# Routing products of a PEER layer: four fp32 matmuls per group of four tokens become twelve bf16 matmuls

## The reference, cut to what matters

```python
experts = i1 * PEER_NKEYS + i2
g = jax.nn.softmax(top_s.astype(jnp.float32), axis=-1)
u = expert_u[ec]
act = jax.nn.gelu(jnp.einsum('cd,ced->ce', xc, u).astype(jnp.float32))
return jnp.einsum('ce,ced->cd', gc * act, expert_v[ec])
```

## Time and profile before

| | |
|---|---|
| median of 3 runs | 1339.16 us |
| the profiled execution | 1341.18 us |
| its span, first to last instruction | 1339.4 us |
| PE busy | 1248.0 us, 93% |
| DVE, ACT, POOL busy | 836.9, 713.1, 564.2 us |
| granted TensorE clock, mean | 0.969 of full speed |
| HBM read and written | 235.36 and 13.11 MB |

### The profile page before, as it was taken

How to read it: one execution, slowest core, us unless ns; L and a number is a source line. 1 busy time by engine, 2 the same in 40 slices (tenths; PEclk the granted TensorE clock), 3 DMA queues, 4 the chain that set the end, 5 groups by cost and what they waited for, 6 DMA issues and landing times.

```text
span 1339.4 us, 26686 instructions
## 1 busy us (share of the span) xinstructions
PE 1248.0 (93%) x8546; PEld 1143.3 (85%) x8546; DVE 836.9 (62%) x1812; ACT 713.1 (53%) x1473; POOL 564.2 (42%) x500
## 2 busy tenths in 40 slices
PE   7979989978898888999999999999999999999996
PEld 6968878976786688999999999999988888888885
DVE  4595766977535544799445555553076767676765
ACT  5435667433545544555664444545555655555554
POOL 2653453532325723788886666667900000000000
PEclk8999999988898988999999999999999999999998
DMA  6575655564453423455555556565757565757552
GB/s 215 168 234 165 221 178 189 191 241 149 167 195 111 142 98 123 156 178 185 172 173 178 186 174 189 179 190 180 259 190 251 203 243 196 252 190 257 195 190 92
DMA packets 85471, 249.35 MB, mean 186 GB/s; under 512 B 7931, under 2 KB 29563, under 8 KB 84508
## 3 DMA queue, kind: packets, MB, share of 16 engines
q1 hardware_dynamic: 77212, 209.69, 47.0%
q0 software_dynamic: 8192, 38.80, 8.3%
HBM read 235.36 MB, written 13.11 MB: 186 GB/s over the span
## 4 chain that ended last, share of the span: by engine, by line
PE 80%; DVE 9%; ACT 4%; issue 3%; POOL 2%; DMA 2%; DVEq 0%; ACTq 0%; SPq 0%
PE psum L626 79%; DVE s_sb L1519 2%; POOL arena L1449 2%; DMA arena<-mods 1%; ACT w_hi L1049 1%; DVE w_lo L1510 1%; ACT arena L1186 1%; PE psum L789 1%; DVE arena L1739 1%; DVE rstd L1504 1%; DVE arena L1625 1%; DMA par<-params 0%; DVE h_lo L1632 0%; DVE h_lo L1546 0%; ACT arena L1032 0%
## 5 line engine op out<-in xcount | busy, mean ns | idle before, releaser
L1049 ACT ACTIVATE w_hi<-ring 128x512 fp32r<-128x512 f32 x734 | 453.6, 631 | 400.9 <-PE psum L626 394.7
L1383 POOL TENSOR_TENSOR w_lo<-ring,w_hi 128x512 fp32r<-128x512 f32 x367 | 483.7, 1321 | 306.5 <-ACT w_hi L1049 294.1
L626 PE MATMUL psum<-h_hi,w_hi 128*128 128x256 f32 x1832 | 540.2, 295 | 44.1 <-DVE w_lo L1510 18.5
L626 PE MATMUL psum<-h_lo,w_hi 128*128 128x256 f32 x1832 | 523.9, 286 | 0.0
L626 PE MATMUL psum<-h_hi,w_lo 128*128 128x256 f32 x1832 | 523.6, 286 | 0.0
L626 PEld LDWEIGHTS psum<-h_hi,w_hi 128*128 128x128 f32 x1832 | 356.8, 195 | 63.9 <-issue 37.3
L626 PEld LDWEIGHTS psum<-h_lo,w_hi 128*128 128x128 f32 x1832 | 357.8, 195 | 0.3
L626 PEld LDWEIGHTS psum<-h_hi,w_lo 128*128 128x128 f32 x1832 | 356.8, 195 | 0.0
L1510 DVE TENSOR_TENSOR w_lo<-ring,w_hi 128x512 fp32r<-128x512 f32 x239 | 182.1, 762 | 138.6 <-ACT w_hi L1049 138.4
L626 PE MATMUL psum<-w_hi,h_hi 128*128 128x512 f32 (+1 forms) x592 | 224.2, 379 | 6.2 <-DVE arena L1527 5.4
L626 PE MATMUL psum<-w_hi,h_lo 128*128 128x512 f32 (+1 forms) x592 | 222.9, 377 | 0.0
(11 more groups left out here) (183 smaller groups left out, 1016.9 us busy)
## 6 DMA issues: line engine op xcount, KB each, us to landing
ring<-u_t SPq DMA_DIRECT2D x128, 512.0 KB, 3.5
ring<-v_rows SPq DMA_DIRECT2D x128, 512.0 KB, 3.5
ring<-weights SPq DMA_DIRECT2D x115, 512.0 KB, 4.0
arena<-mods POOLq DMA_DIRECT2D x48, 512.0 KB, 4.6
routing_weights<-s_sb SPq DMA_DIRECT2D x32, 320.0 KB, 4.2
s_sb<-routing_weights POOLq DMA_DIRECT2D x5, 2048.0 KB, 9.2
bias_rows<-arena POOLq DMA_DIRECT2D x1, 1536.0 KB, 5.9
xres<-x_t SPq DMA_DIRECT2D x1, 1024.0 KB, 4.8
```

What stands on the lines that cost most here:

```text
L626: return nc.tensor.matmul(out, lhs, rhs, start=start, stop=stop, **kw)
L1049: nc.scalar.activation(w_hi[:, half, :], src, ACT.Copy).then_inc(hi_done, 1)
L1383: nc.gpsimd.tensor_tensor(w_lo[:, half, :], src, w_hi[:, half, :].bitcast(F32), ALU.subtract)\
```

## The change: what it does

The routing products are done in bf16. A one-hot row is exact in bf16. The weight is cut into three bf16 pieces that add up to it, so that G = hot1^T x wgt0 + hot1^T x wgt1 + hot1^T x wgt2, accumulated in PSUM: twelve bf16 matmuls a quad, each with 128 columns of weights and 128 moving columns. Once, after the indices are turned, DVE makes the three pieces of all weights in seven instructions; two of them stay in PSUM bank 5, the third goes to SBUF. For each quad DVE makes hot2 (a new table with a one at `i2`) and hot1, and multiplies hot2 by the first and the second piece: four instructions on four tokens each, of which all read an operand in PSUM. ACT multiplies hot2 by the third piece, one instruction a token (`third_weights`), between the gelu and the copy of its step. PE waits for one semaphore more before a quad, and ACT waits for hot2.

```diff
-        hot1 = flat(112, 4).rearrange("p (b t k) -> p b t k", b=2, t=4)
-        wgt = flat(116, 4).rearrange("p (b t k) -> p b t k", b=2, t=4)
-        sel_2, sel_w = s_sb[:, 0:T], s_sb[:, T:2 * T]
+        def quad_pair(region):
+            return region.bitcast(BF16).rearrange("p (b t k) -> p b t k", b=2, t=4)
+
+        hot1, hot2 = quad_pair(flat(112, 2)), quad_pair(flat(114, 2))
+        wgt = [quad_pair(r) for r in (flat(116, 2), flat(118, 2), s_sb[:, 2304:2816])]
+        sel_1, sel_2 = psum[:, 4, 0:T], psum[:, 4, T:2 * T]
+        sel_w = [psum[:, 5, T * x:T * x + T] for x in range(2)]
+        sel_w2, high_part, rest = (s_sb[:, T * x:T * x + T] for x in (0, 2, 3))
+        piece = s_sb[:, T:T + T // 2].bitcast(BF16)
@@ PE
             def quad(s, q, first):
                 pe_.wait_ge(hot1_ready, q + 1)
                 pe_.wait_ge(wgt_ready, q + 1)
+                pe_.wait_ge(wgt2_ready, q + 1)
                 if not first:
                     pe_.wait_ge(g_read, q - 3)
                 for j in range(4):
-                    last = mm(psum[:, GBANKS[s], j * P:j * P + P], hot1[:, s % 2, j, :], wgt[:, s % 2, j, :], True, True)
+                    for x in range(3):
+                        last = mm(psum[:, GBANKS[s], j * P:j * P + P], hot1[:, s % 2, j, :], wgt[x][:, s % 2, j, :], x == 0, x == 2)
                 last.then_inc(route_done, 1)
@@ ACT
+            act.wait_ge(sel_read, 6)
+
+            def third_weights(s, q):
+                act.wait_ge(hot2_ready, q + 1)
+                for t in range(4):
+                    col = sel_w2[:, 4 * q + t:4 * q + t + 1] if isinstance(q, int) else sel_w2[:, bass.ds(q * 4 + t, 1)]
+                    last = nc.scalar.activation(wgt[2][:, s % 2, t, :], hot2[:, s % 2, t, :], ACT.Copy, scale=col)
+                last.then_inc(wgt2_ready, 1)
...
                 for s in range(4):
                     high_u(s, it * 4 + s, False)
                     gelu(s + 2, it * 4 + s - 2)
+                    third_weights(s, it * 4 + s - POOL_TILES)
                     copy_quad(s, it * 4 + s - first, it - first // 4)
@@ DVE
-            v.tensor_copy(sel_2, psum[:, 4, T:2 * T]).then_inc(sel_read, 1)
-            v.tensor_copy(sel_w, psum[:, 5, 0:T]).then_inc(sel_read, 1)
+            v.tensor_copy(piece, sel_w[0]).then_inc(sel_read, 1)
+            dve.wait_ge(sel_read, 1)
+            v.tensor_copy(high_part, piece).then_inc(sel_read, 1)
             dve.wait_ge(sel_read, 2)
+            v.tensor_tensor(rest, sel_w[0], high_part, ALU.subtract).then_inc(sel_read, 1)
+            dve.wait_ge(sel_read, 3)
+            v.tensor_copy(sel_w[0], high_part)
+            v.tensor_copy(piece, rest).then_inc(sel_read, 1)
+            dve.wait_ge(sel_read, 4)
+            v.tensor_copy(sel_w[1], piece).then_inc(sel_read, 1)
+            dve.wait_ge(sel_read, 5)
+            v.tensor_tensor(sel_w2, rest, sel_w[1], ALU.subtract).then_inc(sel_read, 1)
+            dve.wait_ge(sel_read, 6)
...
             def one_hots(q):
                 if q >= 2:
                     dve.wait_ge(route_done, q - 1)
-                rows = iota[:, :].unsqueeze(1).to_broadcast([P, 4, P])
-                v.tensor_tensor(hot1[:, q % 2, :, :], rows, bc(psum[:, 4, 4 * q:4 * q + 4].unsqueeze(2), [P, 4, P]), ALU.is_equal)\
-                    .then_inc(hot1_ready, 1)
-                for t in range(4):
-                    at = 4 * q + t
-                    last = v.tensor_scalar(wgt[:, q % 2, t, :], iota[:, :], sel_2[:, at:at + 1], sel_w[:, at:at + 1],
-                                           ALU.is_equal, ALU.mult)
+                v.tensor_tensor(hot2[:, q % 2, :, :], rows, spread(sel_2, q), ALU.is_equal).then_inc(hot2_ready, 1)
+                v.tensor_tensor(hot1[:, q % 2, :, :], rows, spread(sel_1, q), ALU.is_equal).then_inc(hot1_ready, 1)
+                dve.wait_ge(hot2_ready, q + 1)
+                for x in range(2):
+                    last = v.tensor_tensor(wgt[x][:, q % 2, :, :], hot2[:, q % 2, :, :], spread(sel_w[x], q), ALU.mult)
                 last.then_inc(wgt_ready, 1)
```

More of the change, by code:

```diff
@@ L377, in block_program @@
         wgt_ready = sem("wgt_ready")
+        hot2_ready = sem("hot2_ready")
+        wgt2_ready = sem("wgt2_ready")
         early_weighted = sem("early_weighted")
@@ L1292, in _ @@
             nc.scalar.activation(blk(106), blk(106), ACT.Exp).then_inc(soft_exp, 1)
-            u_loop(SOFT_TILE, POOL_TILES + COPY_LAG)
-            act.wait_ge(sel_done, 1)
+            u_loop(SOFT_TILE, POOL_TILES)
+            act.wait_ge(sel_read, 6)
[5 more added lines that the diff above has]
+                last.then_inc(wgt2_ready, 1)
+            for s in range(COPY_LAG):
+                high_u(s, POOL_TILES + s, False)
+                gelu(s + 2, POOL_TILES + s - 2)
+                third_weights(s, s)
             def copy_quad(s, q, more):
@@ L1307, in _ @@
                 gelu(s + 2, first + s - 2)
+                third_weights(s, COPY_LAG + s)
                 copy_quad(s, s, None)
-            with act.Fori(first // 4 + 1, (first + QUADS) // 4) as it:
+            with act.Fori(first // 4 + 1, (POOL_TILES + QUADS) // 4) as it:
                 for s in range(4):
@@ L1312, in _ @@
                     gelu(s + 2, it * 4 + s - 2)
+                    third_weights(s, it * 4 + s - POOL_TILES)
                     copy_quad(s, it * 4 + s - first, it - first // 4)
+            for s in range(COPY_LAG):
+                n = POOL_TILES + QUADS + s
+                high_u(s, n, False)
+                gelu(s + 2, n - 2)
+                copy_quad(s, n - first, (n - first) // 4)
             u_loop(first + QUADS, P)
@@ L1889, in _, with spread @@
             dve.wait_ge(sel_done, 1)
-            v.tensor_copy(sel_2, psum[:, 4, T:2 * T]).then_inc(sel_read, 1)
-            v.tensor_copy(sel_w, psum[:, 5, 0:T]).then_inc(sel_read, 1)
+            v.tensor_copy(piece, sel_w[0]).then_inc(sel_read, 1)
+            dve.wait_ge(sel_read, 1)
+            v.tensor_copy(high_part, piece).then_inc(sel_read, 1)
             dve.wait_ge(sel_read, 2)
+            v.tensor_tensor(rest, sel_w[0], high_part, ALU.subtract).then_inc(sel_read, 1)
[7 more added lines that the diff above has]
+            dve.wait_ge(sel_read, 6)
+            def spread(row, q):
+                return bc(row[:, 4 * q:4 * q + 4].unsqueeze(2), [P, 4, P])
+            rows = iota[:, :].unsqueeze(1).to_broadcast([P, 4, P])
             def one_hots(q):
```

## The result

The changed kernel takes 1327.63 us (median of 4 runs, 1326.21 to 1329.58) against 1339.68 of before, 12.05 us less; the ratio of the runs is 0.9915 with a 95% interval of 0.9901 to 0.9929. Forecast were 1328.2 us and 11.0 us less, within 1322 to 1345. In a second comparison it took 1328.42 (6 runs) against 1339.05 (19 runs): 0.9922, 0.9906 to 0.9938. All ratios are of undisturbed executions; two of the kernel before, of 2436 and 3942 us, stay out of them.

The account below looks back on a forecast made before the run. PE was taken to bound the kernel: 64 quads at 0.72 instead of 0.89 us save 11.0, the helpers cost nothing. 1341.18 profiled becomes 1330.2, and with the median 2.0 lower, 1328.2 us; range 1322 to 1345.

Parts of the forecast that it names:

- PE sets the pace, and the saving of a quad comes out whole: In the stage from 676.09 us, PE time saved is saved at the end: quad 0.89 to 0.72, 11.0 us in all.
- The price of a pair, 0.060: On PE, one bf16 matmul costs 0.0533 for its columns plus 0.0068; 12 make a quad of 0.72 us.
- fp32r's fixed part: On PE, 0.0135 us of each fp32r matmul beyond its columns; half, 0.0068, was taken for bf16.
- The bounds, columns alone and all of the fixed part: PE's quad at 0.64 us, saving 16.2, with none of the fixed part; at 0.80, saving 5.8, with all.
- VectorE is covered, by 0.75 a step: DVE needs 2.85 us a quad against PE's step of 3.60, so its added work costs nothing.
- the 0.2 for waits: Allowance in DVE's sum per quad, about 0.2 us for the two waits it can meet.
- rival 3: DVE products at 1.05 need 3.76 a step, or ACT above 3.7; time stays 1339; 12% together with a pair near 0.074.
- ScalarE's wait and its lag: ACT idles 1 us for hot2, third pieces add 1.2, high parts start late, POOL ends about 1 us later; cost nothing.
- Once per kernel: DVE prepares the pieces in seven instructions, 2.9 instead of 0.8 us, hidden by five tiles before quad 0.
- Rivals 1 and 2: PE's bf16 weight loads cost 0.112 each, as fp32 (1368 us, 15%), or go by bytes, 0.079 (1342.7 us, 9%).
- What was to show it: Timeline signs: quad near 0.72, step near 3.60, DVE idle about 0.8, ACT waiting about 1 us, chain one piece of PE.

Follow-up runs that it names:

- the half-column kernel: The changed kernel with the second and third piece multiplied for only 64 of 128 moving columns; 1316.84 us against 1338.04 of the kernel before, 0.9831.
- the kernel without this lag: The changed kernel with the third weighted piece made by VectorE instead of ScalarE; 1327.44 us against 1339.05 of the kernel before, 0.993.

## Why the prediction was right

*PE sets the pace, and the saving of a quad comes out whole.* Right: a quad holds PE 0.159 less and the step is 0.153 shorter, 9.8 us in the stage, and the kernel with the new tables but fp32 matmuls gains nothing. The median fell by 12.05 where 11.0 were forecast, and by 10.6 in the second comparison; how near 1328.2 the first came is in part the spread of executions.

*The price of a pair, 0.060.* The sum was right, the working only in part, and that it came out is luck. The pair costs 0.056: the 0.0533 of the columns and hardly anything more. I had added half of fp32r's fixed part, 0.0068, with the reason that bf16 weights have half the bytes; what is there is 0.003, and the half-column kernel shows that the load of bf16 weights, at most 0.028, is not what bounds the pair. Against that, I had nothing for the crossing between fp32r and bf16, which is 0.06 a quad: 0.054 at its end, where the last matmul holds PE for 0.110 instead of 0.056, and 0.01 at its start. Rows 5 had the figure that fits the end, 0.112 for a load that nothing hides, but I looked for it only in the quad's own loads. 12 x 0.004 too much and 0.062 too little nearly cancel: 0.72 forecast, 0.734 measured, 11.0 us forecast and 9.8 in the stage. The bounds, columns alone and all of the fixed part, held.

One reading in it is less certain than it was put: that the fp32 quad was bound by its loads and not by its columns. The kernel before also has fp32 matmuls with 256 moving columns on 128 weight columns:

```profile
219.71 4.55 PE L626 MATMUL psum<-arena,ring 128*128 128x256 f32 x20 [0.18 <-ACT arena L1032]
...
219.71 4.99 PE L626 MATMUL psum<-arena,ring 128*128 128x256 f32 x22 [0.18 <-ACT arena L1032]
```

These are two views of one stretch, and two records more are 0.44: about 0.22 a record (0.216 by the records). If such a record goes by its columns, 128 of them take half of it, 0.108, nearly the 0.112 of the load, so the rows leave open which of the two bound the quad. The forecast does not use it, as a bf16 pair escapes both.

The Trainium skill's page "TensorE: Matmul & The Clock Gate", section "Back-to-back issue gap", has 56 ns for the matmul alone and 81 ns for the pair of load and matmul; this trace agrees with the first (0.056) and not with the second, although every one of these matmuls has its own load of weights. The other rule weighed, the fast load for weights that are not fp32 (section "Weight-path perf modes"), fits the 0.028 measured with 64 moving columns, where fp32 records with 128 weight columns and only 8 moving ones take 0.112.

*VectorE is covered, by 0.75 a step.* Right: 0.87 left, and the four table instructions run at 0.68 like hot1. Of the 0.2 for waits half was needed: 3.61 - 0.87 is 2.74, beside the 2.64 of the instructions. With two products more DVE's own step is 3.85 and the gain is gone, so rival 3 was a real one, two instructions away. Its price, 1.05 for a product with two SBUF operands, came from a misread row; where such a product did run beside POOL, it took 1.04, of which about 0.36 is time that it waited and could spare, so the step held. How much more than this DVE could carry was not tried.

*ScalarE's wait and its lag.* Right in kind and size: 0.70 of waiting where I had 1.0, third pieces of 1.28 where I had 1.2, the high parts late by about a microsecond and POOL with them, and nothing of it reaches PE, whose step is the same in the kernel without this lag.

*Once per kernel.* In the timeline of DVE the seven instructions take 3.1 us and are hidden: from the first matmul that turns the indices to the first quad are 15.04 us in the traces before and after.

*Rivals 1 and 2*, a load bound at 0.112 or 0.079 a pair, are refuted by the pairs of 0.056 and 0.028.

*What was to show it* came as said in the quads, the step and the waits of DVE and ACT, and was wrong in one point. I expected the chain of waits to stay one piece of PE. After the change it runs over POOL for half of this stretch, with "issue" between, where POOL waits for ACT in each step. It names two loops of the same length, of which only PE's is full (60.00 of 60.00 us). The kernel with the third piece on DVE has ACT and POOL earlier and the same step; by the chain alone one would have sped up POOL for nothing.

## What to carry to other kernels

Small fp32 matmuls cost 0.112 us a record with 128 weight columns, two records a matmul, with 8 moving columns as with 128; three bf16 matmuls of exact pieces can be cheaper (3 x 0.056 against 2 x 0.112), and two cheaper still if 16 bits do. Before such a trade, count per step what the engines that make the operands have left, in distances from start to start and not in durations: here a step of 2.74 fitted and one of 3.85 did not. A helper's step that equals that of the bound engine need not be its own pace: a wait can be hidden in a duration, as in the product that ends when POOL lets it. And count what the engine pays on going back to the old kind of work. Take the gain from the stage that changed, since single executions of this kernel begin that stage up to 5.6 us apart.

## What the runs showed of the hardware that was not expected

- A bf16 matmul of 128x128 weights costs 0.056 us with 128 moving columns and 0.028 with 64, each with its own load of weights.
- Going from fp32r to bf16 matmuls and back costs PE 0.065 us each time, at the end of a tile and in the middle of one. The last bf16 matmul ahead of the fp32r ones holds PE for 0.110, with 64 moving columns as with 128, and the first one starts the next 0.066 later instead of 0.056. A second crossing in a tile cost 0.04 net, since the tile's own matmuls then came a little closer together.
- A bf16 DVE product of 128x512 with both operands in SBUF, started while POOL makes a low part, ended 0.55 us (0.57 once) after that low part, in all 64 quads, and so lasted from 0.68 to 1.43 us; POOL's next low part took 1.5 to 1.6 instead of 1.28. With one operand in PSUM the same product took 0.67 to 0.68, beside a busy POOL or not.
